# Masking three chunk matrices of a delta-rule recurrence: on VectorE out of PSUM, or copied by ScalarE and masked by GpSimd

## The chip, the cores and the metric

The kernel runs on one core of a Trainium2 chip. A core has TensorE (matrix products into PSUM), VectorE, ScalarE, GpSimd, and SyncE, which here only issues DMAs. GpSimd works only on SBUF in this kernel: what it masks was put there by another engine. The metric is the device time of one execution in microseconds.

## The reference

Two transformer blocks over 256 tokens of width 1024, one after the other, in float32. The first has a gated linear recurrence, a neighbourhood attention, a memory attention and a convolutional feed-forward part. The second has two layers with five feed-forward and attention parts. The change touches one piece of it, the RWKV-7 time mix of the second block's first layer: 16 heads of 64 columns, and per head a 64 x 64 state.

```python
def step(state, inp):
    r_t, w_t, k_t, v_t, kk_t, b_t = inp
    sa = jnp.einsum('bhij,bhj->bhi', state, -kk_t)
    state = (state * w_t[:, :, None, :] + sa[..., None] * b_t[:, :, None, :]
             + v_t[..., :, None] * k_t[:, :, None, :])
    y = jnp.einsum('bhij,bhj->bhi', state, r_t)
    return state, y
```

## The kernel before, in words

The kernel works this recurrence off in 4 chunks of 64 tokens. Within a chunk the steps depend on each other through a triangular matrix, which must be inverted; the inverse and three more 64 x 64 matrices per head and chunk are made first, for all chunks, and then a short serial loop over the chunks uses them. With A, B, K and R the decayed versions of kk, b, k and r (pages 3, 5, 6, 7), the matrices are products of columns of two of them: (B, A) and (A, B), the two triangles that are inverted; (K, A), called M; (B, R), called RB; and (K, R), called RK. M, RB and RK are read only in the serial part. Each must be masked: M keeps what lies strictly above the diagonal (mask `strict`), RB and RK keep the diagonal too (`incl`).

There are 16 heads x 4 chunks = 64 matrices of a kind. A **group** holds the 16 of four heads, as one tile of 128 x 512; groups 0 to 3 are worked off in two **rounds**, groups 0 and 1, then 2 and 3. Of the eight PSUM banks, group g of a round uses banks 0 to 3 (g even) or 4 to 7 (g odd). A round goes like this:

1. TensorE makes the matrices, all by L616 (`chunk_matrices`): `lower_matrices` of both groups (both triangles, into the upper two of the group's banks), `value_matrices` of both (M and RB, into the lower two banks, semaphore `rw_mb`), `read_matrices` of both (RK, over the first triangle, semaphore `rw_rk`, once VectorE has read both triangles, `rw_lx_read`).
2. VectorE runs `first_inverse` for each group, four instructions: L2026 and L2027 mask the two triangles out of PSUM, L2029 and L2031 make the first inverse.
3. ScalarE copies M and RB of both groups, then RK of both, from PSUM to SBUF: L1399, six instructions a round, each adding one to `rw_plain`.
4. Five levels double the size of the inverted blocks. In each level, for both groups in turn: GpSimd masks the level's part of the triangle (L2194, `rw_lm`); TensorE makes the first product, y, into the banks that held M and RB (L653, `invert_y`); ScalarE copies y to SBUF (L1412, `rw_y_sb`); TensorE makes the second product, z, into the banks that held RK (L667, `invert_z`); VectorE subtracts z from the inverse (L2043, `rw_z_sb`).
5. GpSimd masks the copied M, RB and RK in place (L2183), two instructions after its own work of the second, third and fourth level, each adding one to `rw_masked`.

The order on each engine is the order of the code, and each engine waits on semaphores. Three waits on `rw_plain` and one on `rw_masked` tie the matrices to the rest: y of the first level waits until M and RB of its group have been read (`6 * (g // 2) + 2 * (g % 2) + 2`, so two of the round's six for the even group, four for the odd); z of the first level waits for RK of its group (five of six, or six); and the serial part (`value_part`, L695) waits at L774 for all twelve masks. After it come the serial loop over chunks (L705 to L740), the reading (L750), a group norm and the output projection.

Of the kernel before, what the change touches and what calls it, by code (L numbers as in the profile page):

```python
# [26 lines left out]
ALU = mybir.AluOpType  # L27
ACT = mybir.ActivationFunctionType
# [4 lines left out]
KT = D // P  # L33
# [84 lines left out]
hg_sig hg_silu hg_floor hg_log rw_kk lora_mm gm_vvar hg_expo hg_exp hg_gh hg_keys hg_sc hg_kept hg_av  # L118
hg_o hg_sq hg_var hg_varsb hg_std hg_out merged lora_mid lora_out rw_mix rw_act rw_kk2 rw_kksum rw_kkfloor
rw_kkln rw_kkvar rw_bonus_in rw_bonus_sum rw_cum rw_exp rw_dec rw_t rw_t_sb rw_lx rw_mb rw_rk rw_lt rw_lx_read rw_xx  # L120
rw_plain rw_masked rw_lm rw_y rw_y_sb rw_z rw_z_sb rw_rhs0 rw_rhs1 rw_rhs_sb0 rw_rhs_sb1 rw_u0 rw_u1 rw_u_sb0 rw_u_sb1
rw_ds0 rw_ds1 rw_s0 rw_s1 rw_turn rw_yt rw_yt_sb rw_mean rw_cent rw_sq rw_var rw_varsb
rw_std rw_out fin_gain fin_log fin_inv fin_log2 fin_logs fin_std gm_vnorm gm_vstd gm_vout gm_mask gm_mix gm_mixed
""".split()
# [140 lines left out]
def tensor_program(pe, t, s):  # L265
    ps = t.ps
# [245 lines left out]
    for h in range(HG_H):  # L512
        for qb in range(TB):
            for b in range(TB):
                kept = (t.page[14] if b == qb else t.page[15])[:, (h * 2 + b) * P:(h * 2 + b + 1) * P]
# [26 lines left out]
    for bank, i, w in ((4, 3, [[x[:, 0:P] for x in y] for y in first]),  # L542
# [3 lines left out]
        act = mix_parts(t, i)  # L546
# [224 lines left out]
                          R[rows[e], halves(c, n_ // 2)[n_ % 2]])  # L771
        return mm

    pe.wait_ge(s["rw_masked"], 3 * (KT // 2))  # L774
    for g in range(KT // 2):
        pe.wait_ge(s["rw_z_sb"], inv_at(g, len(LEVELS) - 2) + 1)
    for p in range(2):
# [80 lines left out]
    for q in range(8):  # L858
# [4 lines left out]
        for j in range(4):  # L863
            g, b = 2 * q + j // 2, j % 2
# [4 lines left out]
    for q in range(4):  # L869
        n, b = SEG["gm_o"] + q, BLK["gm_o"] + 2 * q  # L870
# [79 lines left out]
def group(page, g):  # L950
    return page[:, g * 512:(g + 1) * 512]


def RW_M(t):
    return t.page[8]


def RW_RB(t):
    return t.page[10]


def RW_RK(t):
    return t.page[11]
# [74 lines left out]
def scalar_program(act, a, t, s):  # L1038
    ps = t.ps
    norms = norm_table(t, s)  # L1040
    f = act.activation
# [349 lines left out]
    for q in range(12):  # L1391
# [1 line left out]
        b, half = q % 4 // 2, q % 2  # L1393
        act.wait_ge(s["rw_t"], q + 1)
        f(dst[:, b * D + half * 512:b * D + (half + 1) * 512], ps[:, 4 + q % 4, :], ACT.Copy).then_inc(s["rw_t_sb"], 1)
    def plain(made, g, bank, col, page):

        act.wait_ge(s[made], g + 1)
        f(group(page, g).rearrange("p (e n) -> p e n", e=2), ps[:, bank:bank + 2, col:col + 256],  # L1399
          ACT.Copy).then_inc(s["rw_plain"], 1)  # L1400

    for g0 in range(0, KT // 2, 2):
        for g in (g0, g0 + 1):
            plain("rw_mb", g, 4 * (g % 2), 0, RW_M(t))
            plain("rw_mb", g, 4 * (g % 2), 256, RW_RB(t))
        for g in (g0, g0 + 1):
            plain("rw_rk", g, 4 * (g % 2) + 2, 0, RW_RK(t))
        for lv in range(len(LEVELS) - 1):
            for g in (g0, g0 + 1):
                bank = 4 * (g % 2)  # L1410
                act.wait_ge(s["rw_y"], inv_at(g, lv) + 1)
                f(rw_product(t, g).rearrange("p (e n) -> p e n", e=2), ps[:, bank:bank + 2, 0:256],  # L1412
                  ACT.Copy).then_inc(s["rw_y_sb"], 1)
# [77 lines left out]
def vector_program(dve, t, s):  # L1491
    ps = t.ps
    norms = norm_table(t, s)
    link = Link(dve, s["dve_chain"])
    ts, tt, stt = dve.tensor_scalar, dve.tensor_tensor, dve.scalar_tensor_tensor
# [526 lines left out]
    def first_inverse(g):  # L2022
# [8 lines left out]
        tt(blocks, folded(t, "diag").unsqueeze(1).broadcast_to([P, 16, CH]), blocks,  # L2031
           ALU.subtract).then_inc(s["rw_xx"], 1)

    for g0 in range(0, KT // 2, 2):
        first_inverse(g0)
        first_inverse(g0 + 1)
        for lv in range(len(LEVELS) - 1):
            for g in (g0, g0 + 1):
                at_ = 0 if lv < len(LEVELS) - 2 else 256
                inv = rw_inverse(t, g).rearrange("p (e n) -> p e n", e=2)[:, :, at_:]  # L2040
                bank = 4 * (g % 2) + 2
                dve.wait_ge(s["rw_z"], inv_at(g, lv) + 1)
                tt(inv, inv, ps[:, bank:bank + 2, at_:], ALU.subtract).then_inc(s["rw_z_sb"], 1)  # L2043
# [103 lines left out]
def pool_program(pool, t, s):  # L2147
    for col, value in ((COL_EPS, EPS), (COL_GN_EPS, GN_EPS)):
        pool.memset(t.stat[:, col:col + 1], value)
    pool.memset(t.zrow[:], 0.0).then_inc(s["zero_row"], 1)  # L2150
    pool.wait_ge(s["consts_in"], 32)
    pool.wait_ge(s["bias_in"], 16 * 4 * NA_H)
    for page in (14, 15):
        table = t.page[page].rearrange("p (n c) -> p n c", c=NA_COLS)
        window = t.const[:, C_WINDOW:C_WINDOW + NA_COLS].unsqueeze(1).broadcast_to([P, 32, NA_COLS])
        pool.tensor_tensor(table, table, window, ALU.add).then_inc(s["bias_ready"], 1)
    for i, (level, hh) in enumerate(HG_STEPS):
        if level == "same":
            continue
        half = slice(hh * 1024, (hh + 1) * 1024)  # L2160
        v = lambda ap: ap.rearrange("p (g two m) -> p g two m", two=2, m=level)
        eg = v(hg_buf(t, i)[0])
        pool.wait_ge(s["hg_exp"], i + 1)
        pool.tensor_tensor(eg[:, :, 0], eg[:, :, 0], v(t.page[2][:, half])[:, :, 0], ALU.mult)
        pool.tensor_tensor(eg[:, :, 1], eg[:, :, 1], v(t.page[3][:, half])[:, :, 1], ALU.mult).then_inc(s["hg_keys"], 1)

    gains, squares = par(t, "gain_fin", 0, KT), par(t, "gain_fin", KT, KT)
    pool.tensor_tensor(gains, par(t, "norm_final", 0, KT), par(t, "ffn1_norm_2", 0, KT), ALU.mult).then_inc(s["fin_gain"], 1)
    pool.tensor_tensor(squares, par(t, "norm_final", 0, KT), par(t, "norm_final", 0, KT), ALU.mult).then_inc(s["fin_gain"], 1)
    pool.wait_ge(s["fin_gain"], 2)  # L2170
    pool.wait_ge(s["hg_gh"], len(HG_STEPS))
    pool.tensor_copy(t.page[3][:, 0:KT * P].rearrange("p (k m) -> p k m", k=KT),
                     squares.unsqueeze(2).broadcast_to([P, KT, P])).then_inc(s["fin_gain"], 1)
    def wide(ap):
        return ap.rearrange("p (n j) -> p n j", j=CH)

    def mask(name):
        return folded(t, name).unsqueeze(1).broadcast_to([P, 8, CH])

    def masked(page, g, name, ready):  # L2180
        pool.wait_ge(s["rw_plain"], ready)
        matrix = wide(group(page, g))
        pool.tensor_tensor(matrix, matrix, mask(name), ALU.mult).then_inc(s["rw_masked"], 1)  # L2183

    for g0 in range(0, KT // 2, 2):
        done = 3 * g0
        for lv in range(len(LEVELS) - 1):
            for g in (g0, g0 + 1):
                if lv == 0:
                    pool.wait_ge(s["rw_lt"], g + 1)  # L2190
                else:
                    pool.wait_ge(s["rw_y"], inv_at(g, lv - 1) + 1)
                m = LEVELS[len(LEVELS) - 2 - lv]
                pool.tensor_tensor(wide(rw_level(t, g)), wide(rw_lower(t, g)), mask(f"upper{m}"),  # L2194
                                   ALU.mult).then_inc(s["rw_lm"], 1)
            if lv == 1:
                masked(RW_M(t), g0, "strict", done + 1)
                masked(RW_RB(t), g0, "incl", done + 2)
            if lv == 2:
                masked(RW_M(t), g0 + 1, "strict", done + 3)  # L2200
                masked(RW_RB(t), g0 + 1, "incl", done + 4)
            if lv == 3:
                masked(RW_RK(t), g0, "incl", done + 5)
                masked(RW_RK(t), g0 + 1, "incl", done + 6)


def constants():
# [133 lines left out]
```

## Time and profile before

| | |
|---|---|
| median of three runs | 2282.19 us (2281.58 to 2287.51) |
| profiled execution, its own time | 2291.96 us |
| its span (first to last instruction) | 2290.2 us |
| busy: TensorE, VectorE, ScalarE, GpSimd | 2025.1, 1371.3, 1054.8, 110.0 us |
| mean granted TensorE clock | 0.934 of full speed |
| the two rounds lie at | 1133 to 1210 us of the span |

The profile is one execution; its times are for durations and order, and differences between kernels are taken from the runs. A timeline row is a run of equal instructions: start, busy time, engine, line, what it writes and reads, how many, and in brackets the idle time before them and who ended it. "issue" there is idle time for which no other instruction is found.

### The profile page before, as it was taken

The page shows a single profiled execution, that of the slowest core. Times are in us where ns is not written, and L with a number is a line of the kernel's source. Part 1 is how long each engine was busy: PE and PEld are TensorE (multiplying, and loading weights), DVE is VectorE, ACT ScalarE, POOL GpSimd, SP SyncE. Part 2 cuts the span into 40 slices and gives each one's busy share as a digit, 9 for nine tenths or more (in the row PEclk, how much of TensorE's full clock was granted, in tenths as well). Part 3 has the DMA queues.
Part 4 walks back from the last instruction along what each step waited for, and adds up shares of the span by engine and source line. Part 5 has one row for each costly group of instructions (what it writes and reads, how often), then busy time and mean ns, then how long its engine had stood idle before and what let it go on. Part 6 is the DMA issues. An engine that isn't in the chain of part 4 may idle for free.

```text
span 2290.2 us, 43344 instructions
## 1 busy us (share of the span) xinstructions
PE 2025.1 (88%) x18123; PEld 1943.1 (85%) x18128; DVE 1371.3 (60%) x1662; ACT 1054.8 (46%) x1314; POOL 110.0 (5%) x76
## 2 busy tenths in 40 slices
PE   6999778758999899978698798999999797979997
PEld 5999448748999899978587797999999797969997
DVE  5454449965777755585842754655655644546555
ACT  5445524533655544454622453544544544435443
POOL 0010004320000000000060000000000000000000
PEclk9999659978999999989798899999999998999998
DMA  5654102203455354434001342445455444324452
GB/s 204 224 185 165 56 0 95 108 19 118 170 191 182 130 184 182 182 108 153 38 4 76 111 162 78 167 182 183 167 183 183 165 148 147 129 93 155 180 181 108
DMA packets 51585, 314.53 MB, mean 137 GB/s; under 512 B 13456, under 2 KB 13584, under 8 KB 13584
## 3 DMA queue, kind: packets, MB, share of 16 engines
q1 hardware_dynamic: 50752, 307.63, 37.3%
q10 hardware_dynamic: 720, 5.24, 0.6%
q8 instruction: 90, 1.47, 0.3%
q14 instruction: 23, 0.19, 0.0%
HBM read 311.80 MB, written 1.05 MB: 137 GB/s over the span
## 4 chain that ended last, share of the span: by engine, by line
PE 79%; DVE 12%; ACT 5%; issue 2%; DMA 1%; POOL 0%; ACTq 0%; SPq 0%; DVEq 0%
PE ps L272 68%; DVE wl L1506 2%; PE ps L442 2%; PE ps L421 2%; PE ps L667 1%; DVE work L1529 1%; PE ps L507 1%; ACT wh L1053 1%; PE ps L431 1%; PE ps L418 1%; PE ps L653 1%; DVE h_r L1558 1%; PE ps L616 1%; DMA raw<-in_stream 1%; DVE pages L1762 1%
## 5 line engine op out<-in xcount | busy, mean ns | idle before, releaser
L1506 DVE TENSOR_TENSOR wl<-raw,wh 128x1024 fp32r<-128x1024 f32 x576 | 714.6, 1252 | 590.7 <-ACT wh L1053 588.3
L1053 ACT ACTIVATE wh<-raw 128x1024 fp32r<-128x1024 f32 x576 | 601.0, 1053 | 589.3 <-PE ps L272 548.8
L272 PE MATMUL ps<-sq_r,wh 128*128 128x256 f32 x2592 | 741.8, 286 | 25.9 <-DVE h_r L1523 8.3
L272 PE MATMUL ps<-sq_r,wl 128*128 128x256 f32 x2592 | 736.8, 284 | 0.0
L272 PE MATMUL ps<-h_r,wh 128*128 128x256 f32 x2560 | 726.6, 284 | 0.0
L272 PE MATMUL ps<-pages_r,wh 128*128 128x256 f32 x2480 | 550.9, 288 | 66.3 <-DVE pages_r L1523 57.1
L272 PEld LDWEIGHTS ps<-sq_r,wh 128*128 128x128 f32 x2592 | 501.4, 193 | 30.0 <-issue 16.3
L272 PEld LDWEIGHTS ps<-sq_r,wl 128*128 128x128 f32 x2592 | 501.2, 193 | 0.0
L272 PEld LDWEIGHTS ps<-h_r,wh 128*128 128x128 f32 x2560 | 493.6, 193 | 0.4
L272 PEld LDWEIGHTS ps<-pages_r,wh 128*128 128x128 f32 x2480 | 429.1, 197 | 70.4 <-issue 60.4
L272 PE MATMUL ps<-pages_r,wl 128*128 128x256 f32 x1680 | 481.3, 286 | 0.0
L272 PEld LDWEIGHTS ps<-pages_r,wl 128*128 128x128 f32 x1680 | 328.9, 196 | 0.0
L272 PE MATMUL ps<-work_r,wh 128*128 128x256 f32 x976 | 273.1, 286 | 0.0
L272 PEld LDWEIGHTS ps<-work_r,wh 128*128 128x128 f32 x976 | 188.6, 196 | 0.0
L1264 ACT ACTIVATE pages_r<-work 128x512 fp32r<-128x512 f32 x55 | 34.7, 632 | 152.1 <-DVE work L1928 124.0
L507 PE MATMUL ps<-pages 128*128 128x128 f32 x288 | 46.5, 329 | 35.9 <-DVE pages L1762 28.0
L507 PEld LDWEIGHTS ps<-pages 128*128 128x128 f32 x288 | 43.4, 239 | 38.8 <-DVE pages L1762 30.1
L272 PE MATMUL ps<-wh,h_r 128*128 128x256 f32 x224 | 63.4, 283 | 0.0
L272 PE MATMUL ps<-wh,sq_r 128*128 128x256 f32 x224 | 63.4, 283 | 0.0
L272 PE MATMUL ps<-wl,sq_r 128*128 128x256 f32 x224 | 63.4, 283 | 0.0
L1334 ACT ACTIVATE work<-work 128x512 f32<-128x512 f32 x44 | 27.8, 632 | 75.9 <-DVE work L1573 75.9
L1820 DVE TENSOR_TENSOR work_r<-work,pages_r 128x512 fp32r<-128x512 f32 x55 | 38.1, 692 | 38.4 <-ACT pages_r L1264 38.4
(260 smaller groups left out, 1964.8 us busy)
## 6 DMA issues: line engine op xcount, KB each, us to landing
raw<-in_stream SPq DMA_DIRECT2D x288, 1024.0 KB, 4.8
pages<-in_rpb SPq DMA_DIRECT2D x32, 64.0 KB, 5.4
const<-in_consts SPq DMA_DIRECT2D x1, 1184.0 KB, 7.9
pages<-in_mem SPq DMA_DIRECT2D x1, 1024.0 KB, 5.1
x<-in_x SPq DMA_DIRECT2D x1, 1024.0 KB, 13.7
pages<-in_mem ACTq DMA_DIRECT2D x1, 1024.0 KB, 5.6
pages<-in_gmlp_b ACTq DMA_DIRECT2D x1, 1024.0 KB, 7.7
pages<-in_gmlp_gain ACTq DMA_DIRECT2D x1, 1024.0 KB, 9.1
```

The costliest lines, as they stand in the source:

```text
L272: mm = pe.matmul(out, left, right, start=start and q == 0, stop=stop and q == 2, skip_group_check=True)
L418: pe.matmul(ps[:, 4 + g % 2, qb * 256:(qb + 1) * 256], cst(t, "flip"), bias(h, qb), start=True, stop=False, skip_group_check=True)
L421: mm = pe.matmul(ps[:, 4 + g % 2, qb * 256:(qb + 1) * 256], q(h, c)[:, qb * P:(qb + 1) * P], k(h, c), start=c == 0 and not bias, stop=c == ...
L431: mm = pe.transpose(ps[:, 6, mb * 256 + qb * P:mb * 256 + (qb + 1) * P], att_buf(t, g)[:, qb * 256 + mb * P:qb * 256 + (mb + 1) * P], cst( ...
L442: mm = pe.matmul(ps[dst_rows(h), 7, c * T:(c + 1) * T], v(h, c, mb), att_turned(t, g)[:, mb * T:(mb + 1) * T], start=mb == 0, stop=mb == T ...
L507: mm = pe.matmul(ps[:, 4 + 2 * (i % 2) + j // 4, (j % 4) * P:(j % 4 + 1) * P], keys[:, h * T + b * P:h * T + (b + 1) * P], queries[:, h * ...
L616: mm = pe.matmul(ps[rows[par], bank + e, at_:at_ + CH], left[rows[e], tok], right[rows[e], tok], start=True, stop=True)
L1053: f(t.wh[(2 * b0 + hf) % PIECE_SLOTS][:], t.raw[b0 % 2][:, hf * 1024:(hf + 1) * 1024], ACT.Copy).then_inc(s["high_done"], 1)
L1264: f(hidden_parts(t, k)[0], t.work[:, k * 512:(k + 1) * 512], ACT.Copy).then_inc(s["hidden_high"], 1)
L1334: f(gate_, gate_, ACT.Silu).then_inc(s["gate_ready"], 1)
L1506: tt(t.wl[i][:], t.raw[b0 % 2][:, hf * 1024:(hf + 1) * 1024], t.wh[i][:].bitcast(F32), ALU.subtract).then_inc(s["low_done"], 1)
L1820: tt(low_, t.work[:, k * 512:(k + 1) * 512], high_.bitcast(F32), ALU.subtract).then_inc(s["hidden_ready"], 1)
```

## The change

ScalarE's six copies a round and GpSimd's six masks a round are taken out. VectorE gets six multiplications a round instead (`kept`, L2026 of the changed code), each from PSUM times the mask into the page in SBUF, placed behind the two `first_inverse` of the round and ahead of the levels. They are in the order of the copies (M and RB of the even group, M and RB of the odd one, RK of both) and add to `rw_plain`, so TensorE's waits in the first level keep their numbers. The wait at L774 is now for twelve on `rw_plain`.

```diff
--- before.py
+++ after.py
@@ -118,7 +118,7 @@
 hg_sig hg_silu hg_floor hg_log rw_kk lora_mm gm_vvar hg_expo hg_exp hg_gh hg_keys hg_sc hg_kept hg_av
 hg_o hg_sq hg_var hg_varsb hg_std hg_out merged lora_mid lora_out rw_mix rw_act rw_kk2 rw_kksum rw_kkfloor
 rw_kkln rw_kkvar rw_bonus_in rw_bonus_sum rw_cum rw_exp rw_dec rw_t rw_t_sb rw_lx rw_mb rw_rk rw_lt rw_lx_read rw_xx
-rw_plain rw_masked rw_lm rw_y rw_y_sb rw_z rw_z_sb rw_rhs0 rw_rhs1 rw_rhs_sb0 rw_rhs_sb1 rw_u0 rw_u1 rw_u_sb0 rw_u_sb1
+rw_plain rw_lm rw_y rw_y_sb rw_z rw_z_sb rw_rhs0 rw_rhs1 rw_rhs_sb0 rw_rhs_sb1 rw_u0 rw_u1 rw_u_sb0 rw_u_sb1
 rw_ds0 rw_ds1 rw_s0 rw_s1 rw_turn rw_yt rw_yt_sb rw_mean rw_cent rw_sq rw_var rw_varsb
 rw_std rw_out fin_gain fin_log fin_inv fin_log2 fin_logs fin_std gm_vnorm gm_vstd gm_vout gm_mask gm_mix gm_mixed
 """.split()
@@ -771,7 +771,7 @@
                           R[rows[e], halves(c, n_ // 2)[n_ % 2]])
         return mm
 
-    pe.wait_ge(s["rw_masked"], 3 * (KT // 2))
+    pe.wait_ge(s["rw_plain"], 3 * (KT // 2))
     for g in range(KT // 2):
         pe.wait_ge(s["rw_z_sb"], inv_at(g, len(LEVELS) - 2) + 1)
     for p in range(2):
@@ -1393,18 +1393,7 @@
         b, half = q % 4 // 2, q % 2
         act.wait_ge(s["rw_t"], q + 1)
         f(dst[:, b * D + half * 512:b * D + (half + 1) * 512], ps[:, 4 + q % 4, :], ACT.Copy).then_inc(s["rw_t_sb"], 1)
-    def plain(made, g, bank, col, page):
-
-        act.wait_ge(s[made], g + 1)
-        f(group(page, g).rearrange("p (e n) -> p e n", e=2), ps[:, bank:bank + 2, col:col + 256],
-          ACT.Copy).then_inc(s["rw_plain"], 1)
-
     for g0 in range(0, KT // 2, 2):
-        for g in (g0, g0 + 1):
-            plain("rw_mb", g, 4 * (g % 2), 0, RW_M(t))
-            plain("rw_mb", g, 4 * (g % 2), 256, RW_RB(t))
-        for g in (g0, g0 + 1):
-            plain("rw_rk", g, 4 * (g % 2) + 2, 0, RW_RK(t))
         for lv in range(len(LEVELS) - 1):
             for g in (g0, g0 + 1):
                 bank = 4 * (g % 2)
@@ -2031,9 +2020,19 @@
         tt(blocks, folded(t, "diag").unsqueeze(1).broadcast_to([P, 16, CH]), blocks,
            ALU.subtract).then_inc(s["rw_xx"], 1)
 
+    def kept(ready, g, bank, j, page, name):
+
+        dve.wait_ge(s[ready], g + 1)
+        tt(view(group(page, g)), made(bank, j), mask(name), ALU.mult).then_inc(s["rw_plain"], 1)
+
     for g0 in range(0, KT // 2, 2):
         first_inverse(g0)
         first_inverse(g0 + 1)
+        for g in (g0, g0 + 1):
+            kept("rw_mb", g, 4 * (g % 2), 0, RW_M(t), "strict")
+            kept("rw_mb", g, 4 * (g % 2), 1, RW_RB(t), "incl")
+        for g in (g0, g0 + 1):
+            kept("rw_rk", g, 4 * (g % 2) + 2, 0, RW_RK(t), "incl")
         for lv in range(len(LEVELS) - 1):
             for g in (g0, g0 + 1):
                 at_ = 0 if lv < len(LEVELS) - 2 else 256
@@ -2177,13 +2176,7 @@
     def mask(name):
         return folded(t, name).unsqueeze(1).broadcast_to([P, 8, CH])
 
-    def masked(page, g, name, ready):
-        pool.wait_ge(s["rw_plain"], ready)
-        matrix = wide(group(page, g))
-        pool.tensor_tensor(matrix, matrix, mask(name), ALU.mult).then_inc(s["rw_masked"], 1)
-
     for g0 in range(0, KT // 2, 2):
-        done = 3 * g0
         for lv in range(len(LEVELS) - 1):
             for g in (g0, g0 + 1):
                 if lv == 0:
@@ -2193,15 +2186,7 @@
                 m = LEVELS[len(LEVELS) - 2 - lv]
                 pool.tensor_tensor(wide(rw_level(t, g)), wide(rw_lower(t, g)), mask(f"upper{m}"),
                                    ALU.mult).then_inc(s["rw_lm"], 1)
-            if lv == 1:
-                masked(RW_M(t), g0, "strict", done + 1)
-                masked(RW_RB(t), g0, "incl", done + 2)
-            if lv == 2:
-                masked(RW_M(t), g0 + 1, "strict", done + 3)
-                masked(RW_RB(t), g0 + 1, "incl", done + 4)
-            if lv == 3:
-                masked(RW_RK(t), g0, "incl", done + 5)
-                masked(RW_RK(t), g0 + 1, "incl", done + 6)
+
 
 
 def constants():
```

VectorE's queue in the first round, from the second group's `first_inverse` on; before:

```order
L2026 TENSOR_TENSOR pages<-ps,const 128x512 [waits rw_lx]
L2027 TENSOR_TENSOR pages<-ps,const 128x2x256
L2029 TENSOR_TENSOR pages<-pages,const 128x2x256 [waits rw_lt]
L2031 TENSOR_TENSOR pages<-const,pages 128x1024 [waits dve_chain]
L2043 TENSOR_TENSOR pages<-pages,ps 128x1024 [waits rw_z] x8
L2043 TENSOR_TENSOR pages<-pages,ps 128x2x256 [waits rw_z] x2
```

and now (its lines moved up by 11, so L2015 to L2020 are the former L2026 to L2031, L2042 is the former L2043, and L2026 is new):

```order
L2015 TENSOR_TENSOR pages<-ps,const 128x512 [waits rw_lx]
L2016 TENSOR_TENSOR pages<-ps,const 128x2x256
L2018 TENSOR_TENSOR pages<-pages,const 128x2x256 [waits rw_lt]
L2020 TENSOR_TENSOR pages<-const,pages 128x1024 [waits dve_chain]
L2026 TENSOR_TENSOR pages<-ps,const 128x512 [waits rw_mb] x4
L2026 TENSOR_TENSOR pages<-ps,const 128x512 [waits rw_rk] x2
L2042 TENSOR_TENSOR pages<-pages,ps 128x1024 [waits rw_z] x8
L2042 TENSOR_TENSOR pages<-pages,ps 128x2x256 [waits rw_z] x2
```

Six multiplications now stand between the last instruction of `first_inverse` and the first subtraction of the levels, four behind `rw_mb` and two behind `rw_rk`.

GpSimd's queue, from the last instruction ahead of the rounds, through the first round; before:

```order
L2172 COPY pages<-param 128x1024 [waits hg_gh,fin_gain]
L2194 TENSOR_TENSOR sq<-pages,const 128x512 [waits rw_lt] x2
L2194 TENSOR_TENSOR sq<-pages,const 128x512 [waits rw_y] x2
L2183 TENSOR_TENSOR pages<-pages,const 128x512 [waits rw_plain] x2
L2194 TENSOR_TENSOR sq<-pages,const 128x512 [waits rw_y] x2
L2183 TENSOR_TENSOR pages<-pages,const 128x512 [waits rw_plain] x2
L2194 TENSOR_TENSOR sq<-pages,const 128x512 [waits rw_y] x2
L2183 TENSOR_TENSOR pages<-pages,const 128x512 [waits rw_plain] x2
L2194 TENSOR_TENSOR sq<-pages,const 128x512 [waits rw_y] x2
L2194 TENSOR_TENSOR sq<-pages,const 128x512 [waits rw_lt] x2
```

and now, both rounds:

```order
L2171 COPY pages<-param 128x1024 [waits hg_gh,fin_gain]
L2187 TENSOR_TENSOR sq<-pages,const 128x512 [waits rw_lt] x2
L2187 TENSOR_TENSOR sq<-pages,const 128x512 [waits rw_y] x8
L2187 TENSOR_TENSOR sq<-pages,const 128x512 [waits rw_lt] x2
L2187 TENSOR_TENSOR sq<-pages,const 128x512 [waits rw_y] x8
```

The pairs of masks (L2183) are gone from between the level masks (now L2187).

## Rows read from the trace of the kernel before

**Rows 1.** The page: the chain that ended last, by engine.

```profile
...
PE 79%; DVE 12%; ACT 5%; issue 2%; DMA 1%; POOL 0%; ACTq 0%; SPq 0%; DVEq 0%
...
```

**Rows 2.** TensorE's timeline: start, us, engine, line, operation, out<-in, count [idle before <-releaser].

```profile
...
1140.23 2.73 PE L616 MATMUL ps<-pages 64*64 64x64 f32 x92 [2.94 <-issue]
1142.65 0.31 PE L653 MATMUL ps<-pages,sq 64*64 64x64 f32 x1
...
1145.02 1.15 PE L667 MATMUL ps<-sq,pages 64*64 64x64 f32 x32
...
1150.28 1.15 PE L653 MATMUL ps<-pages,sq 64*64 64x64 f32 x32 [0.38 <-DVE pages L2043]
1151.26 1.10 PE L667 MATMUL ps<-sq,pages 64*64 64x64 f32 x32
...
1175.53 2.10 PE L616 MATMUL ps<-pages 64*64 64x64 f32 x128 [1.22 <-issue]
1178.99 0.74 PE L616 MATMUL ps<-pages 64*64 64x64 f32 x35 [1.37 <-issue]
1179.52 0.22 PE L653 MATMUL ps<-pages,sq 64*64 64x64 f32 x1
...
1183.03 0.38 PE L667 MATMUL ps<-sq,pages 64*64 64x64 f32 x5 [0.43 <-issue]
...
1210.04 3.85 PE L695 MATMUL ps<-pages 64*64 64x64 f32 x125 [0.88 <-DVE pages L2043]
...
```

**Rows 3.** The same for VectorE, both rounds.

```profile
...
1137.31 1.23 DVE L2031 TENSOR_TENSOR pages<-const,pages 128x1024 f32<-128x1024 f32 x1
1138.45 0.68 DVE L2026 TENSOR_TENSOR pages<-ps,const 128x512 f32<-128x512 f32 x1
1139.05 0.68 DVE L2027 TENSOR_TENSOR pages<-ps,const 128x512 f32<-128x512 f32 x1
...
1141.06 1.23 DVE L2031 TENSOR_TENSOR pages<-const,pages 128x1024 f32<-128x1024 f32 x1
...
1155.21 1.22 DVE L2043 TENSOR_TENSOR pages<-pages,ps 128x1024 f32<-128x1024 f32 x1 [0.65 <-PE ps L667]
...
1179.36 1.23 DVE L2031 TENSOR_TENSOR pages<-const,pages 128x1024 f32<-128x1024 f32 x1
...
1186.26 1.22 DVE L2043 TENSOR_TENSOR pages<-pages,ps 128x1024 f32<-128x1024 f32 x1 [0.65 <-PE ps L667]
...
```

**Rows 4.** The same for ScalarE.

```profile
...
1141.40 2.30 ACT L1399 ACTIVATE pages<-ps 128x512 f32<-128x512 f32 x4 [3.52 <-PE ps L616]
1144.28 0.60 ACT L1412 ACTIVATE sq<-ps 128x512 f32<-128x512 f32 x1 [0.57 <-PE ps L653]
...
1179.36 1.08 ACT L1399 ACTIVATE pages<-ps 128x512 f32<-128x512 f32 x2 [0.93 <-PE ps L616]
1180.76 0.60 ACT L1412 ACTIVATE sq<-ps 128x512 f32<-128x512 f32 x1 [0.32 <-PE ps L653]
...
```

**Rows 5.** The same for GpSimd (POOL).

```profile
...
1144.33 2.49 POOL L2194 TENSOR_TENSOR sq<-pages,const 128x512 f32<-128x512 f32 x2 [3.85 <-PE ps L653]
1146.77 2.50 POOL L2183 TENSOR_TENSOR pages<-pages,const 128x512 f32<-128x512 f32 x2
...
1196.20 2.50 POOL L2183 TENSOR_TENSOR pages<-pages,const 128x512 f32<-128x512 f32 x2
...
```

**Rows 6.** One line, L2043: durations in ns, smallest, median and largest.

```profile
...
L2043 DVE TENSOR_TENSOR pages<-pages,ps x20: 686/1220/1221, 1147.1 to 1209.2; 128x1024 f32<-128x1024 f32 x16, 128x512 f32<-128x512 f32 x4
...
```

**Rows 7.** Stretches: length; busy us (instructions) per engine; granted clock; DMA share, GB/s.

```profile
...
1138.00:1140.00 2.00, 0.00 (x0) 0.00 (x0) 2.00 (x4) 0.00 (x0) 0.79 (x1) 1.00 0.02 8
1140.00:1142.00 2.00, 1.77 (x67) 1.77 (x68) 1.97 (x2) 0.60 (x2) 0.48 (x1) 0.52 0.03 8
1143.00:1144.00 1.00, 1.00 (x33) 1.00 (x30) 0.00 (x0) 0.60 (x1) 0.00 (x0) 0.75 0.00 0
...
1171.80:1179.50 7.70, 5.12 (x321) 4.83 (x320) 7.12 (x9) 2.20 (x5) 2.53 (x2) 1.00 0.02 4
...
```

## The prediction

> **What bounds the kernel now.** I read the page's first and fourth parts, then asked the trace for the chain of waits and the timeline of each engine over the only stretch that the change touches. The chain that ended last is 79% TensorE and 12% VectorE; GpSimd, busy for 110.0 us by the table of the time before, has 0% of it [rows 1]. So work taken from GpSimd is worth something only where somebody waits for it.
>
> The stretch runs from 1133 to 1210 us and holds two rounds, groups 0 and 1, then groups 2 and 3. I call the steps of a group by their lines: L616 makes the chunk matrices, L653 the first product of a level (y), L667 the second (z). Inside the levels TensorE is nearly full: y of the round's second group starts at 1150.28, its z group follows 0.98 later, and VectorE's subtraction at L2043 finds z finished at 1155.21; with L2043's own 1.22 and some 0.05 until the next y that is a period of 6.20 us, in which TensorE idles 0.38 [rows 2, 3]. Neither ScalarE nor GpSimd ends a wait of TensorE there. The start of a round is different: VectorE works without a break through the eight instructions L2026 to L2031, and in the second round y of group 3 can only start when the last of them ends, 1179.36 + 1.23 = 1180.59 [rows 3]. VectorE is the engine that sets the second round's start already, and it is where the change puts its work.
>
> **What is removed.** ScalarE loses 12 copies at L1399, six a round: four in 2.30 us from 1141.40, two in 1.08 us from 1179.36 [rows 4]. None stands in the way: ScalarE copies the first y of group 0 at 1144.28, when y has just ended, and the copies before it ended at 1143.70; in round two they ended at 1180.44 and the first y copy starts at 1180.76 [rows 4]. Gain 0. GpSimd loses 12 masks at L2183, in pairs of 2.50 us behind two L2194 [rows 5]. Could an L2194 come sooner? In a level GpSimd has two of them and two masks, 2.49 + 2.50 of 6.20 us [rows 5], so the queue is empty again before the next y; and the L653 that reads an L2194 comes only after both z groups. Gain 0. The last masks end at 1196.20 + 2.50 = 1198.70, while the value matrices that wait for all of them (L774, L695) start at 1210.04, after a wait that VectorE's L2043 ended [rows 2, 5]. Gain 0 as well.
>
> Could the masks slow VectorE from the side? Of the 20 L2043, some run wholly beside masks, others (the fourth level's) with none, and their 128x1024 form has a median of 1220 and a maximum of 1221 ns [rows 6]. Gain 0.
>
> **What is added.** 12 multiplications on VectorE, PSUM times a mask in `const`, 128x512. It is exactly the form of L2026 and L2027, so I need no bound from elsewhere: 0.68 us long, and the next one starts 0.60 us after (1138.45 to 1139.05) [rows 3]. After L2031 the next instruction starts 1.14 us after it (1137.31 to 1138.45) [rows 3]. Round 1: L2031 of group 1 starts at 1141.06, so the six start at 1142.20, 1142.80, 1143.40, 1144.00, 1144.60 and 1145.20. Their inputs are there: the copies of group 1 began at 1141.40, so its matrices were ready [rows 4]. In the worst case six an entire round are exposed: 6 × 0.60 = 3.6 us a round, 7.2 in all. In the best case none. Which of the six does TensorE wait for? y of a group overwrites the banks of the first two matrices, so it waits for two of them (g even) or four (g odd); z waits for the fifth or sixth.
>
> Round 1, in the clock of the profile. RB of group 0 ends 1142.80 + 0.68 = 1143.48; y of group 0 starts about 0.05 later, 1143.53 instead of 1142.65 [rows 2]. RB of group 1 ends at 1144.68, its y starts at 1144.73. From the second y to the first z is 0.98, so z of group 0 starts at 1145.71, against 1145.02: **0.69 us late**. The fifth and sixth masks end at 1145.28 and 1145.88, before their z; the y copy (it starts 1.24 after y, as at 1180.76, and is 0.60 long [rows 2, 4]) is ready at 1145.37. None adds more.
>
> Round 2. The six start at 1179.36 + 1.14 = 1180.50, then 1181.10, 1181.70, 1182.30, 1182.90, 1183.50. RB of group 2 ends 1181.78, y starts 1181.82 instead of 1179.52. RB of group 3 ends 1182.98, its y starts 1183.03. z of group 2 starts 1184.01; the L2043 of group 3 comes 3.95 us after that (1151.26 to 1155.21), 1187.96, against 1186.26: **1.70 us late** [rows 2, 3]. The first z was late already in the profile, by an "issue" gap of 0.43 us at 1183.03, and I take that gap to be passed by then. If it comes again the term is 2.13.
>
> What is that gap? TensorE's gaps without a releaser end at 1140.23 (2.94 us), 1175.53 (1.22), 1178.99 (1.37) and 1183.03 (0.43), and from the second to the third are exactly 128 matmuls, each with its weight load [rows 2]. That is the picture of instructions that arrive late in equal blocks, and a stream that is slower by itself gives them time. The Trainium skill, in "Runtime: NRT & Kernel Launch", section "Instruction fetch mechanics", says that the sequencer fetches blocks of 256 instructions ahead and that this is mostly hidden. The block size agrees with 128 matmuls and 128 weight loads here, the hiding does not, with 2.94 us in one gap; had the page been right on that, the 0.43 would have another cause and the sum would be 0.43 higher.
>
> Sum: 12 masks at 0.60 are 7.2 us of VectorE time; of it 4.8 lie beside y, z and the wait for them, **0.69 + 1.70 = 2.4 us** on the path. Everything later in the layer hangs on this chain (L695 waits for L2043) and moves by as much. The profiled execution took 2291.96 us for a span of 2290.2, so its own forecast is 2294.4. The three runs have a median of 2282.19, 9.8 us less, and the profiled stage is 2.4 us longer either way: **2284.6 us**, 0.1% more. About 0.3%, 6.8 us, is what a measurement of this kernel can tell from no change.
>
> **Rivals.**
> 1. TensorE falls to half clock in the second round. The granted clock was 1.00 until 1140, with TensorE idle from 1137.3 to 1140.2, and 0.52 right after, which is the lower level, 1.2 GHz; between 1143 and 1144 its mean is 0.75, so it rose again there, about 3.5 us later [rows 7]. The new wait makes TensorE idle from about 1179.7 to 1181.8, behind gaps of 1.22 and 1.37 us that did not lower it (1.00 throughout) [rows 7]. Price: y of group 0, most of it at the lower level, took 1.63 us to its copy, y of group 2 at the full one 1.24 [rows 2, 4], 31% more; over 3.5 us of such a stretch that is about 1 us, 2 if it lasts twice that. Total 3.4 to 4.4, time 2286.1. Against it: the new idle time is shorter than the one that did it. The Trainium skill, in "TensorE: Matmul & The Clock Gate", section "HAM oscillation — how this bites in real kernels", says that pauses between bursts of matmuls put the array back to its slow rate; the trace agrees at 1140 and not at 1175 and 1179. [...]
> 2. All twelve are exposed: 7.2 us, with a low-clock stretch of 1.0 about 8.2, time 2290.4, slower. It happens if VectorE bounds the round right through, which needs z to wait for the sixth mask or L2043 to queue behind it by more than it does now. For it: VectorE is busy 7.12 of 7.70 us before the second round's levels [rows 7]. Against it: the sixth ends at 1184.18, and the L2043 behind it would start two z groups later. It decides once a mask takes more than about twice 0.60 us.
> 3. The delay is given back: z of both rounds catches up because instructions arrive late anyway, or because the second round's VectorE work starts no later. That needs y of group 2 to be bound by something else at 1181.8, and nothing in the trace is. 2282.2.
> 4. Faster: the half-clock stretches of the rest fall otherwise. In round 1 such a stretch cost about 1 us (rival 1), and a program shifted by 2.4 us may miss or meet others later. To end 0.3% faster it must win 2.4 + 6.8 = 9.2 us that way, nine stretches: 2275.4.
>
> **How the numbers follow.** The forecast, 2.4 us late, 0.60; rival 1, 0.20; rival 2, 0.10; rival 3, 0.06; rival 4, 0.04. Within 0.3%: 0.60 + 0.20 + 0.06 = 0.86. Slower 0.10, faster 0.04. Range: from the no-cost case less the 0.6 us that the fastest run lay under the median, with about 1.1 us for the median's own scatter, 2280.5; up to rival 2's 2290. The likeliest case alone is 2283 to 2287.
>
> **What would show it.** VectorE must have 12 new rows of 0.68 us, starts 0.60 apart, six right behind each second L2031. TensorE must show a new wait for VectorE before the second round's first L653, about 2.1 us, and y starts 0.9 and 2.3 us later against the L2031 before them. Level periods stay 6.20, L2043 stays 1.22. GpSimd's busy time falls by 12 × 1.25 = 15 us and ScalarE's by about 7, without anything starting sooner. The granted clock from 1180 to 1187 decides rival 1. I am wrong if the new instructions take over 0.8 us, if TensorE waits for the sixth of them, or if the stage grows by less than 1.5 or more than 4 us.

## The result, and the profile after

| | before | after |
|---|---|---|
| median of 10 runs, same chip | 2285.91 us (2281.58 to 2287.99) | 2291.59 us (2288.13 to 2294.35) |
| profiled execution, span | 2291.96 us, 2290.2 us | 2288.13 us, 2286.3 us |
| VectorE, ScalarE, GpSimd busy | 1371.3, 1054.8, 110.0 us | 1378.9, 1048.5, 95.4 us |

The measured ratio is 1.0029, 95% interval 1.0019 to 1.0039: 4.3 to 8.9 us slower, about 0.3%; the medians themselves lie 5.7 us apart. The forecast was 2.4 us slower and 2284.6 us, in a range from 2280.5 to 2290; the measured 2291.59 lies 1.6 us above it. Of the 7.0 us between that and 2291.59, 3.7 lie in the base (the three runs that the forecast started from had a median of 2282.19, the ten have 2285.91) and 3.3 in the difference.

The profiled executions go the other way, 2288.13 against 2291.96, so the span of one execution says nothing here; the stage has to be read by itself. First the page of the changed kernel: busy us, share and instructions of each engine, then the chain that ended last.

```profile
PE 2018.9 (88%) x18123; PEld 1938.7 (85%) x18128; DVE 1378.9 (60%) x1674; ACT 1048.5 (46%) x1302; POOL 95.4 (4%) x64
...
PE 79%; DVE 13%; ACT 5%; issue 2%; DMA 1%; POOL 0%; ACTq 0%; SPq 0%; DVEq 0%
```

The work moved as forecast (VectorE +7.6, ScalarE −6.3, GpSimd −14.6 us), and the chain gained VectorE from 12 to 13% [rows 1]. Next TensorE's timeline of the changed kernel, with the columns of [rows 2].

```profile
1140.14 2.83 PE L616 MATMUL ps<-pages 64*64 64x64 f32 x94 [2.92 <-issue]
1143.52 2.34 PE L653 MATMUL ps<-pages,sq 64*64 64x64 f32 x64 [0.55 <-issue]
1145.67 1.13 PE L667 MATMUL ps<-sq,pages 64*64 64x64 f32 x32
...
1148.69 1.09 PE L667 MATMUL ps<-pages,sq 64*64 64x64 f32 x31
...
1176.10 2.10 PE L616 MATMUL ps<-pages 64*64 64x64 f32 x128 [0.92 <-issue]
1179.84 0.80 PE L616 MATMUL ps<-pages 64*64 64x64 f32 x36 [1.64 <-issue]
1182.76 3.68 PE L653 MATMUL ps<-pages,sq 64*64 64x64 f32 x64 [2.12 <-issue]
1186.20 1.85 PE L667 MATMUL ps<-sq,pages 64*64 64x64 f32 x32
1187.86 1.12 PE L667 MATMUL ps<-pages,sq 64*64 64x64 f32 x32
...
1214.67 3.54 PE L695 MATMUL ps<-pages 64*64 64x64 f32 x114 [0.88 <-DVE pages L2042]
```

And VectorE's timeline beside it; its line numbers are 11 lower than before, and L2026 is the new line.

```profile
1137.24 1.23 DVE L2020 TENSOR_TENSOR pages<-const,pages 128x1024 f32<-128x1024 f32 x1
...
1142.14 3.67 DVE L2026 TENSOR_TENSOR pages<-ps,const 128x512 f32<-128x512 f32 x6
...
1149.88 1.22 DVE L2042 TENSOR_TENSOR pages<-pages,ps 128x1024 f32<-128x1024 f32 x1 [0.89 <-PE ps L667]
...
1180.24 1.23 DVE L2020 TENSOR_TENSOR pages<-const,pages 128x1024 f32<-128x1024 f32 x1
1181.38 3.67 DVE L2026 TENSOR_TENSOR pages<-ps,const 128x512 f32<-128x512 f32 x6
...
1190.88 1.22 DVE L2042 TENSOR_TENSOR pages<-pages,ps 128x1024 f32<-128x1024 f32 x1 [0.64 <-PE ps L667]
```

Read them together. The second mask of the round, RB of group 2, starts at 1181.38 + 0.60 and ends at 1182.66; y starts at 1182.76. The trace calls the 2.12 us before it "issue", but it is the wait for VectorE: in the first round the same two ends lie 0.10 apart as well (1142.14 + 0.60 + 0.68 = 1143.42, y at 1143.52). Against the L2020 or L2031 of the second group, y of the second round starts after 2.52 us instead of 0.16 [rows 2, 3]: 2.36 late, forecast 2.30.

Then the row that was not forecast: these 64 matmuls take 3.68 us, those of the first round 2.34. The stretches of the changed kernel (columns as in [rows 7]) say why.

```profile
1180.60:1181.00 0.40, 0.04 (x1) 0.00 (x0) 0.40 (x1) 0.00 (x0) 0.00 (x0) 0.96 0.00 0
1181.00:1182.76 1.76, 0.00 (x0) 0.03 (x1) 1.76 (x4) 0.00 (x0) 0.00 (x0) 0.50 0.01 5
1182.80:1184.80 2.00, 2.00 (x38) 2.00 (x40) 2.00 (x4) 0.03 (x1) 0.00 (x0) 0.50 0.03 8
1184.80:1186.80 2.00, 2.00 (x44) 2.00 (x42) 0.25 (x1) 0.89 (x2) 1.55 (x2) 0.50 0.00 0
```

The granted clock is at its lower level, 1.2 GHz, in the whole of y. The kernel before had 1.00 up to 1179.50 [rows 7] and has 1.00 in the z groups too:

```profile
1183.60:1184.60 1.00, 1.00 (x40) 1.00 (x38) 0.21 (x1) 0.00 (x0) 1.00 (x2) 1.00 0.08 16
```

It did not fall at the end of the wait: it is down from 1181.0 on, when TensorE had been idle for only 0.4 us of the new 2.12 (0.7 in e8, the second profile of this kernel).

From y to the first z there are 3.44 us instead of 2.11, and the first z group takes 1.66 to the next instead of 0.93. The rest of the levels runs at the old pace.

To compare kernels I measure one stage in each profile. R1 is the first round, from its first L2026 (or the line that took its place) to the first L2043 of its second group; R2 is the same of the second round; "rounds" is from that first instruction of round 1 to the last L2043. A second profiled execution of each kernel, e8 and e11, gave the same numbers within 0.1 us.

| | R1 | R2 | rounds | clock in the six 1-us stretches from the second round's first y |
|---|---|---|---|---|
| before | 14.33 | 13.27 | 74.53 | 1.00 |
| before again (e11) | 14.29 | 13.20 | 74.44 | 1.00 |
| after | 15.27 | 17.01 | 79.22 | 0.50 five times, 0.98 |
| after again (e8) | 15.27 | 17.02 | 79.22 | 0.50 five times, 0.98 |

So the change costs 0.94 + 3.74 = 4.7 us there, against 0.69 + 1.70 forecast.

### The profile page after: what moved, and what is told of

Read it like the earlier page. It is cut to its first block, busy times and chain, and to the rows that moved or that the text cites. A ratio compares the mean times of both kernels' runs of the same rounds, so it can differ in the third digit from the quotient of the medians.

```text
span 2286.3 us, 43332 instructions
## 1 busy us (share of the span) xinstructions
PE 2018.9 (88%) x18123; PEld 1938.7 (85%) x18128; DVE 1378.9 (60%) x1674; ACT 1048.5 (46%) x1302; POOL 95.4 (4%) x64
## 4 chain that ended last, share of the span: by engine, by line
PE 79%; DVE 13%; ACT 5%; issue 2%; DMA 1%; POOL 0%; ACTq 0%; SPq 0%; DVEq 0%
PE ps L272 68%; DVE wl L1495 2%; PE ps L442 2%; PE ps L421 2%; PE ps L667 2%; DVE work L1518 1%; PE ps L507 1%; ACT wh L1053 1%; PE ps L431 1%; PE ps L653 1%; PE ps L418 1%; DVE pages L1751 1%; DMA raw<-in_stream 1%; DVE h_r L1547 0%; ACT pages L1180 0%
```

## The experiments

Two theories. **A**: the mechanism is as forecast, only masks that y waits for are exposed, and what is above 2.4 us is TensorE's lower clock after the new wait. **B**: VectorE's longer queue bounds the round more deeply, and the clock has little to do with it. Each expectation says what the two mean for its run; there B stands for whatever else could cause the loss in it.

**e1 and e2, one round at a time.** Before, with the new masks in one round only (e1: round 1, e2: round 2). The edit of e1, shortened; in e2 the two conditions are exchanged, the RK copies and GpSimd's masks have the same guards, and L774 waits for both sorts of masks:

```diff
-        for g in (g0, g0 + 1):
-            plain("rw_mb", g, 4 * (g % 2), 0, RW_M(t))
+        if g0 == 2:
+            for g in (g0, g0 + 1):
+                plain("rw_mb", g, 4 * (g % 2), 0, RW_M(t))
...
+        if g0 == 0:
+            for g in (g0, g0 + 1):
+                kept("rw_mb", g, 4 * (g % 2), 0, RW_M(t), "strict")
```

> Only groups 0 and 1 are masked by VectorE out of PSUM; groups 2 and 3 keep ScalarE's copies and GpSimd's masks. Theory A (the loss is VectorE's queue at the start of a round, plus a half-clock stretch that the longer wait in round 2 brings): the first round's last first-level subtraction comes 0.7 to 0.9 us later than before, round 2 stays as before with the full clock, L695 about 0.9 us later, time +0.9 us (0.04%), same. Theory B (the loss is spread over both rounds and the rest of the kernel, clock in round 2 falls anyway): about half of the 5.7 us, +2.8, and the clock of round 2's first level low here too.

> Only groups 2 and 3 are masked by VectorE out of PSUM. Theory A: round 2's first product starts some 2.3 us later, TensorE idles 2.1 us before it, the granted clock falls to 0.5 for the first level, the first level ends 3.7 us later than before (1.7 if the clock stays up), time +3.7 us (0.16%). Theory B: +2.8 us, and L695 no more than 2 us late.

e1: rounds 75.80 (+1.3, 0.9 expected), R1 15.55, clock 1.00 in round 2; ratio 1.0009 [0.9995, 1.0023]. In its first round a z group that was due at 1145.95 starts at 1146.47; without that R1 would be 0.70 over before, as expected. e2: rounds 78.71 (+4.2, 3.7 expected), R2 17.44, with the clock down until 1185.9; ratio 1.0028 [1.0017, 1.0040]. Most of the cost is the second round's, and there TensorE's timeline of e2 has the same slow y:

```profile
1177.34 0.80 PE L616 MATMUL ps<-pages 64*64 64x64 f32 x36 [1.64 <-issue]
1179.96 3.68 PE L653 MATMUL ps<-pages,sq 64*64 64x64 f32 x64 [1.82 <-issue]
1183.40 1.95 PE L667 MATMUL ps<-sq,pages 64*64 64x64 f32 x32
```

**e3, the clock alone.** The changed kernel, with 16 matmuls put into the second round's wait, whose results nobody reads. The RK mask of group 2 waits for them besides (semaphore `rw_fill`); they have ended by then, and VectorE's six masks run on without a gap.

```diff
+    def fill(g, n):
+        for k in range(n):
+            par, e = k // 2 % 2, k % 2
+            mm = pe.matmul(ps[rows[par], 4 * (g % 2) + 2 + e, 256:512], B[rows[e], 0:CH], A[rows[e], 0:256],
+                           start=True, stop=True)
+        mm.then_inc(s["rw_fill"], 1)
...
             stage(g + 1)
+        if g:
+            fill(g, 16)
```

> The changed kernel with 16 filler matmuls (64x256, into halves of PSUM banks whose content has been read, results unused) on TensorE in the wait ahead of round 2's first product. Theory A (idle time lowers the clock): the granted clock stays at 1.00 through round 2's first level, that level's two products and two second products take 5.5 instead of 7.5 us, L695 some 2 us earlier than in the changed kernel, time 2 us (0.1%) less than it, so +3.6 over before. Theory B (clock falls for another reason, or the filler takes as long as the wait and delays the block of instructions behind it): no gain, or a further 0.5 to 1 us.

TensorE's timeline of e3; L674 is the filler:

```profile
1178.99 0.74 PE L616 MATMUL ps<-pages 64*64 64x64 f32 x35 [1.63 <-issue]
...
1179.62 1.89 PE L674 MATMUL ps<-pages 64*64 64x256 f32 x29
1181.95 2.34 PE L653 MATMUL ps<-pages,sq 64*64 64x64 f32 x64 [0.43 <-issue]
1184.09 1.13 PE L667 MATMUL ps<-sq,pages 64*64 64x64 f32 x32
```

```profile
1182.80:1184.80 2.00, 1.95 (x68) 1.84 (x65) 1.43 (x3) 1.07 (x2) 1.62 (x2) 1.00 0.02 4
```

y starts where it did after (8.90 us after the round's first VectorE instruction; 8.89 there, 6.53 before), but its 64 matmuls take 2.34 us again at a clock of 1.00, and R2 is 15.01. This is the decisive run: at the full clock the second round costs 15.01 − 13.27 = 1.74 us, the forecast's 1.70, and the clock adds 17.01 − 15.01 = 2.00. Theory B falls. The rounds are 77.48 us. The time, 1.0016 [1.0005, 1.0028], does not separate e3 from the changed kernel (1.0029, and 1.0013 in e8 below).

**e4, only RK moved**, with M and RB copied and masked as before. Shortened; RK's masks count on a semaphore of their own, for which z and L774 wait.

```diff
-        for g in (g0, g0 + 1):
-            plain("rw_rk", g, 4 * (g % 2) + 2, 0, RW_RK(t))
...
+        for g in (g0, g0 + 1):
+            kept("rw_rk", g, 4 * (g % 2) + 2, 0, RW_RK(t), "incl")
```

> Only RK goes to VectorE, two masks a round, directly behind first_inverse; M and RB stay with ScalarE and GpSimd. Theory A (only what y of the first level waits for costs): RK of group 1 ends 1.9 us after L2031 starts + 0.4, before z needs it; nothing is late, time as before (within 1 us). Theory B (each VectorE instruction in front of the levels costs its 0.6 us): 4 of them cost 2.4 us, +0.1%.

R2 is 13.35 (+0.08), clock 1.00, y at 6.46: RK's masks are free in the second round. Rounds 75.36 (+0.8), nearly all of it in R1, 15.07: there a z group due at 1150.36 starts at 1151.14, behind a gap of 0.58 us without a releaser. Such gaps of 0.3 to 0.6 us came in the first round of e1, e3, e4, e6 and e7 and not in before. They all stand at the same place: from L616's long gap of that round (2.8 to 3.2 us) to this one there are 254 matmuls in each of the five kernels, and 254 in after too (94 + 64 + 3 × 32), two short of two blocks of 128. So they are gaps of the kind that the prediction describes, and masks on VectorE do not make them: e6 has none in its first round. Time 1.0007 [0.9997, 1.0017].

The second round of e4 is worth a look for the clock. Two gaps, about as long as the first two of after, stand ahead of a y that needs not wait, and the clock is 1.00 in all six stretches from y on.

```profile
1178.51 2.10 PE L616 MATMUL ps<-pages 64*64 64x64 f32 x128 [0.88 <-issue]
1182.24 0.74 PE L616 MATMUL ps<-pages 64*64 64x64 f32 x35 [1.63 <-issue]
1182.77 0.22 PE L653 MATMUL ps<-pages,sq 64*64 64x64 f32 x1
```

e1 (0.83 and 1.64 us) and e6 (1.18 and 1.64) are alike.

**e10, four more instructions.** The changed kernel, RK masked twice, once to a place that is not read.

```diff
+            tt(view(group(t.h[:, :], g)), made(4 * (g % 2) + 2, 0), mask("incl"), ALU.mult).then_inc(s["rw_twice"], 1)
             kept("rw_rk", g, 4 * (g % 2) + 2, 0, RW_RK(t), "incl")
```

> The changed kernel with both RK masks of each round computed twice on VectorE (the second result goes to a scratch tile nobody reads): four more instructions of 0.60 us, behind those that y waits for. Theory A (only what y waits for is exposed): z of the first level is 0.2 us late in round 1 and 0 to 0.2 in round 2, stage +4.7 to +5.1 over before. Theory B (every instruction of VectorE ahead of the levels costs its 0.60): +2.4 more, 7.1 over before.

Rounds 79.49, +0.27 for four instructions of 0.60 us, 2.4 in all. The sum hides two shifts of the clock: R1 is 16.25, since behind a longer gap (3.71 us) the clock was 0.50 up to 1146.50, through both y of the first level, with 3.39 us instead of 2.15 to the first z; and R2 is 16.30, since the clock was down for a shorter part of it. That the two nearly cancel is chance. y of the second round starts at 8.89, as after. Behind what y waits for, VectorE has room. Where they stand in its timeline (L2036 are the extra ones):

```profile
1182.00 2.48 DVE L2026 TENSOR_TENSOR pages<-ps,const 128x512 f32<-128x512 f32 x4
1184.39 0.68 DVE L2036 TENSOR_TENSOR h<-ps,const 128x512 f32<-128x512 f32 x1
1184.99 0.68 DVE L2026 TENSOR_TENSOR pages<-ps,const 128x512 f32<-128x512 f32 x1
1185.59 0.68 DVE L2036 TENSOR_TENSOR h<-ps,const 128x512 f32<-128x512 f32 x1
1186.19 0.68 DVE L2026 TENSOR_TENSOR pages<-ps,const 128x512 f32<-128x512 f32 x1
1188.92 1.22 DVE L2044 TENSOR_TENSOR pages<-pages,ps 128x1024 f32<-128x1024 f32 x1 [2.05 <-PE ps L667]
```

The last ends at 1186.87, and 2.05 us later VectorE still waits for z. Time 1.0020 [1.0008, 1.0031].

**e7, GpSimd's masks back.** The changed kernel, with the 12 GpSimd masks done again on matrices that are masked already, at their old places (the other two pairs follow), and with L774 waiting for them.

```diff
+            if lv == 1:
+                masked(RW_M(t), g0, "strict", done + 1)
+                masked(RW_RB(t), g0, "incl", done + 2)
...
```

> The changed kernel with GpSimd's twelve in-place masks put back behind VectorE's masks (they change nothing in what is already masked), and the serial part waiting for them again. Both theories of the loss: as the changed kernel, within 1 us; stage +4.7 us over before. If the masks on GpSimd had slowed something that the change relieved: 1 us or more slower than the changed kernel.

Rounds 79.24 against 79.22, with R1 15.82 (a gap of 0.30 us at the place that e4 has it, and 2.37 us from y to the first z instead of 2.15) and R2 16.47 (the clock was down for a shorter part). The equal sum is chance, since two shifts of 0.5 us cancel in it; but y of the second round starts at 8.89 in both. Time 1.0015 [1.0002, 1.0029]. GpSimd's masks were worth nothing that these runs can tell. ScalarE's copies were not put back in any run.

**e5 and e6, less VectorE work ahead.** The third instruction of `first_inverse` (L2029) reads the chunk matrix in PSUM instead of the masked copy in SBUF, and comes second; in the changed kernel (e5) and in before (e6):

```diff
+        tt(part[:, :, 1], made(bank, 0), mask("upper1"), ALU.mult)
         tt(part[:, :, 0], made(bank, 1), mask("lower1"), ALU.mult).then_inc(s["rw_lx_read"], 1)
-        dve.wait_ge(s["rw_lt"], g + 1)
-        link(tt(part[:, :, 1], view(lower), mask("upper1"), ALU.mult))
+        dve.wait_ge(s["rw_lx_read"], g + 1)
```

> The changed kernel, with the third instruction of first_inverse (the upper1 part, before L2029) reading the triangle out of PSUM like its two neighbours, not the masked copy in SBUF while GpSimd works on that copy. The values are the same. Theory A (the loss is the length of VectorE's queue ahead of y): each first_inverse takes some 3.0 instead of 3.76 us, 1.6 us a round; round 1 is as before the change; round 2's first product is at most 0.7 us later than before, the clock stays up, stage +0.4 us over before, time within 1 us of before and 5 us under the changed kernel. Theory B (the masks on VectorE cost by being there, or something outside the stage does): still +3 us or more over before.

> The kernel before with the same edit of first_inverse. Theory A: in round 2 y of group 3 waited for L2031 only some 0.15 us longer than for TensorE's own order, and an instruction gap of 0.43 follows; gain 0 to 0.4 us, same. Theory B (VectorE bounds the start of a round): 1.6 us a round, 3.2 us or 0.14% faster.

e5: rounds 75.95, 3.3 us under after, but 1.4 over before where 0.4 was expected (R1 14.04, R2 14.98). TensorE's timeline of e5, and two of its stretches:

```profile
1172.51 2.10 PE L616 MATMUL ps<-pages 64*64 64x64 f32 x128 [0.95 <-issue]
1176.24 0.80 PE L616 MATMUL ps<-pages 64*64 64x64 f32 x36 [1.63 <-issue]
1177.73 3.17 PE L653 MATMUL ps<-pages,sq 64*64 64x64 f32 x64 [0.70 <-issue]
```

```profile
1176.90:1177.70 0.80, 0.14 (x7) 0.00 (x0) 0.80 (x3) 0.00 (x0) 0.00 (x0) 1.00 0.00 0
1178.70:1180.70 2.00, 2.00 (x41) 1.95 (x39) 1.32 (x3) 0.60 (x1) 1.27 (x1) 0.50 0.03 8
```

The wait has shrunk from 2.12 to 0.70 us, and the clock still fell, when y had been running for 0.8 to 1.0 us (1.00 up to 1178.50, 0.50 from 1178.75). Against e4, e1 and e6 the third gap is what is new. e6 gained nothing: R2 13.20, rounds 75.30, and a first round of 15.16, 0.8 longer than before's. Of that, 0.7 is the gap at 254 matmuls, where a z group starts 0.71 us late. Times 1.0007 [0.9997, 1.0016] and 0.9999 [0.9988, 1.0010].

**e9, e5 with a filler.** As in e3, with eight matmuls instead of 16.

> The changed kernel with first_inverse reading PSUM throughout and 8 filler matmuls in round 2's wait (results unused). Theory A: round 2's clock stays at 1.00, its first level ends 13.6 to 13.8 us after the round's first VectorE instruction (13.27 before, 14.98 without the filler), stage +0.3 us over before, time within 1 us of before. If the clock falls for another reason than idle time: 15 us as without the filler.

```profile
1176.76 1.03 PE L674 MATMUL ps<-pages 64*64 64x256 f32 x13
1177.66 2.34 PE L653 MATMUL ps<-pages,sq 64*64 64x64 f32 x64
```

```profile
1178.70:1180.70 2.00, 1.95 (x67) 1.87 (x65) 1.25 (x3) 1.20 (x2) 1.80 (x2) 1.00 0.01 4
```

R2 is 13.62 where 13.6 to 13.8 was expected, rounds 74.85, 0.3 over before. Its median is 2284.71 us against 2286.71, ratio 0.9994 [0.9984, 1.0003]: it cannot be told from the kernel before. Its interval lies below the changed kernel's (1.0019 to 1.0039) and touches e8's (0.9999 to 1.0026).

**e8 and e11, the two kernels again.** No edit.

> The changed kernel once more, for a second profile. Theory A: the granted clock falls to 0.5 at round 2's first product again, and its first level ends 3.7 us later than before counted from the round's first VectorE instruction. Theory B (the low stretch there was chance): clock 1.00 in this profile and 1.7 us.

> The kernel before once more, for a second profile. Its round 1 takes 14.3 us and round 2 13.3 us as in the first profile, clock 1.00 in round 2; the serial part behind the rounds takes 22.3 us as in every other profile, not the 23.4 of the first, whose TensorE clock was low at 1230.

e8: 1.0013 [0.9999, 1.0026]. e11: 1.0006 [0.9994, 1.0018], which is what no change looks like in 12 runs. e11 missed one expectation: from the last L2043 to the end of the serial part I expected 22.3 us, as in the variants, and measured 23.36, as before has it (23.43). Both executions of the kernel before have a low clock in that part, which none of the eleven others has. Before, e11 and after, the same kind of stretch:

```profile
1229.00:1235.00 6.00, 6.00 (x85) 5.89 (x85) 1.89 (x4) 1.18 (x2) 0.00 (x0) 0.50 0.00 0
```

```profile
1226.00:1232.00 6.00, 5.96 (x81) 5.91 (x83) 2.18 (x4) 1.03 (x2) 0.00 (x0) 0.52 0.00 0
```

```profile
1229.00:1235.00 6.00, 5.50 (x132) 4.95 (x127) 3.37 (x7) 1.24 (x3) 0.00 (x0) 1.00 0.01 3
```

So in the profiles 1.1 us of the 4.7 come back right behind the rounds. Then more comes back: from the serial part to the first operand of the next stage before took 39.26 and 40.10 us, after 36.76 and 37.14. By that point the profiles of after have won back 3.6 us (first profiles) and 4.0 (second) of the 4.7. The other variants lie between 36.8 and 39.3 there, e6, which hardly differs from before, at 37.0. The rest of the kernel varies from 1013.4 to 1018.3 us among the 13 profiles.

## Why the prediction was wrong, step by step

- **The additions.** Right. The 12 masks take 678 to 683 ns and start 0.60 apart: VectorE gained 7.6 us, forecast 7.2.
- **Removals at nothing.** Right for GpSimd: e7. For ScalarE it rests on [rows 4] alone, since no run put its copies back.
- **What y waits for.** Right in both rounds. In round 1 the first z starts 8.43 us after the first L2020, against 7.71 before [rows 2, 3]: 0.72 late, forecast 0.69. The other 0.2 of the measured 0.94 is a gap before 1148.69, where the z group was due at 1148.46; it stands at the 254 matmuls of e4. In round 2 the shift at full clock is 1.74 (e3), forecast 1.70, with the 0.43 us gap passed by, as I took it to be.
- **The failed step: rival 1, the clock.** It was named, priced at 1 to 2 us and given 0.20, on the argument that "the new idle time is shorter than the one that did it". It happened, in both executions of the changed kernel and in e2, e5, e7 and e10, at 2.0 us in the changed kernel and 1.3 to 2.4 in the others; it was gone in e3 and e9, where fillers took the idle time. That 2.0 is the upper end of the price is partly luck: the price took 31% more time, from a y that was only partly at the lower level, over 3.5 us, and measured are 57% (64 matmuls in 3.68 us, not 2.34) over 5.0 us. The argument compared one wait with one wait. But the new wait joins two gaps, so that 0.92, 1.64 and 2.12 us follow each other with only short groups of L616 between them, and 0.4 us of the third had passed when the clock fell. e5 shows that 0.95 and 1.63 with a third of only 0.70 suffice, while two such gaps alone do not, in before, e1, e4, e6 and e11. Rival 1's own total was 3.4 to 4.4; the rounds show 4.7. The Trainium skill, in "TensorE: Matmul & The Clock Gate", section "HAM oscillation — how this bites in real kernels", has waits between bursts of matmuls as what puts the array back to its slow rate. The trace of after agrees in kind, 0.50 from 1181.0 on; but the waits of that section's example are longer than these three, so it does not say that a cluster of short ones is enough, and e5 does.
- **Rival 2** (all twelve exposed) is out by e4 and e10, **rival 3** (given back) by the late y. **Rival 4** is half there: a shifted program missed a low-clock stretch in the serial part, for 1.1 us and not for nine such stretches.
- **The time.** The prediction's bound of 4 us for the growth of the stage is passed, with 4.7. The timed difference, 5.7 us [4.3, 8.9] in the first comparison, was 1.0013 in e8; over the four kernels with the full change in the rounds (after, e8, e7, e10) the ratios average 1.0019, 4.4 us. That fits the rounds, 4.7, and so do the rest of the runs: the six comparisons with rounds of 77.5 to 79.5 us (after, e2, e3, e7, e8, e10) average 1.0020, the six with 74.4 to 76.0 (e1, e4, e5, e6, e9, e11) 1.0004, which is 3.8 us apart in time and 3.6 in the rounds. What does not fit is the stretch behind the rounds, where the two profiles of before are 3.6 to 4.0 us longer than those of after; the times show nothing of it, and whether most executions of before have it stays open.
- **Left open:** why the 0.2 to 0.6 us gaps of round 1, which always stand at the same matmul, come in one run and not in another, and why the serial part's clock falls in both profiles of before only.

## What to carry to other kernels

Work moved off an idle engine gains nothing, and put on the engine that a start waits for it costs what stands ahead of the wait: count the instructions ahead, not all of them. A new wait of TensorE must be judged with the gaps that lie around it; look for the granted clock behind the nearest such cluster, and give the fall its full chance. Where that clock is the cost, a few matmuls whose results nobody reads take it back in the wait (2.0 us of the profiled rounds here). The delay of y itself stays. To bring the kernel to where it was took both, the wait shortened at its source and a filler in what was left of it (e9).

## What the runs showed of the hardware

- The granted clock fell with TensorE idle for only 0.70 us behind gaps of 0.95 and 1.63 us (e5). It held where only two gaps stood, of 0.88 and 1.63 us (e4), and with 16 or 8 matmuls of 64x256 in the third (e3, e9).
- It need not fall while TensorE is idle: in e5 it fell 0.8 to 1.0 us after y had started.
- It can be low while TensorE counts as fully busy: 0.50 with 6.00 of 6.00 us busy in the serial part of before, where a group of L730 takes 3.35 us instead of 2.03:

```profile
1225.22 2.03 PE L730 MATMUL ps<-pages 64*64 64x64 f32 x32
...
1230.64 3.35 PE L730 MATMUL ps<-pages 64*64 64x64 f32 x29
```

- Beside a GpSimd mask, the mask of 128x512 takes VectorE 1.38 us when both operands lie in SBUF (before and after), and 0.68 when one lies in PSUM. Before's timeline, then e5's:

```profile
1174.20 1.38 DVE L2029 TENSOR_TENSOR pages<-pages,const 128x512 f32<-128x512 f32 x1
```

```profile
1170.84 0.68 DVE L2016 TENSOR_TENSOR pages<-ps,const 128x512 f32<-128x512 f32 x1
1171.44 0.68 DVE L2017 TENSOR_TENSOR pages<-ps,const 128x512 f32<-128x512 f32 x1
```

  In both kernels GpSimd works at the time, as its timelines show, of before and of e5:

```profile
1173.76 1.26 POOL L2194 TENSOR_TENSOR sq<-pages,const 128x512 f32<-128x512 f32 x1 [8.56 <-DVE pages L2026]
```

```profile
1171.00 1.27 POOL L2187 TENSOR_TENSOR sq<-pages,const 128x512 f32<-128x512 f32 x1 [8.57 <-DVE pages L2015]
```

  SBUF alone doesn't make it slow. In before, a multiplication of the same size with both operands in SBUF takes 0.69 us at 1941 to 1951 us, where GpSimd has nothing to do (ns: smallest, median, largest):

```profile
L2131 DVE TENSOR_TENSOR pages<-work,pages x8: 691/692/692, 1940.9 to 1950.6; 128x512 f32<-128x512 f32 x8
```

  So it is GpSimd beside it, though no run took GpSimd's work away from L2029 itself. VectorE's 1174.20 + 1.38 ends 0.56 us after GpSimd's 1173.76 + 1.26. The Trainium skill, in "SBUF — State Buffer", section "Who interferes with whom", describes a port pair that the two engines share under an exclusive lock; the two durations agree with it.
